# Decay sums of a gated-DeltaNet branch made once and laid out by DMA, with loads and block transfers issued by ScalarE

## What is computed

```python
gc = cumsum(g)                                     # inside the chunk
decay = exp(where(incl, gc[:, None] - gc[None, :], -inf))
kb = k * beta
lmat = where(strict, (kb @ k.T) * decay, 0)
sol = solve_unit_lower(lmat + I, concat([v * beta, kb * exp(gc)]))
u, w = sol[:, :dv], sol[:, dv:]
qk = where(incl, (q @ k.T) * decay, 0)
qg, kg = q * exp(gc), k * exp(gc[-1] - gc)
# per chunk, in order:
v_new = u - w @ s
o = qg @ s + qk @ v_new
s = s * exp(gc[-1]) + kg.T @ v_new
```

## Time and profile before

| | |
|---|---|
| median of 3 runs | 1328.33 us |
| lowest, highest | 1324.12, 1330.24 us |
| profiled execution | 1325.04 us, span 1322.7 us |
| PE busy | 1242.5 us (94% of the span) |
| DVE, ACT, POOL busy | 673.5, 294.7, 436.7 us |
| moved by DMA | 269.28 MB |

### The profile page before, as it was taken

The page is one execution under the profiler, slowest core; times in us unless marked ns, Lnnn a source line. Parts: engine busy times, 40 slices in busy tenths (PEclk is TensorE's granted clock), DMA queues, the critical chain, the costliest instruction groups (busy, mean ns, idle before and its releaser), DMA issues.

```text
span 1322.7 us, 20474 instructions
## 1 busy us (share of the span) xinstructions
PE 1242.5 (94%) x7131; PEld 635.1 (48%) x7131; DVE 673.5 (51%) x961; ACT 294.7 (22%) x650; POOL 436.7 (33%) x232
## 2 busy tenths in 40 slices
PE   6999999999989989999968887878999999999998
PEld 3444444455445444545535453334666644444443
DVE  3666305758878697684536653824442232543010
ACT  3111103333334433333312120001122221110000
POOL 1122203745444445444446654425441100000000
PEclk9999999999999999999989999998999999999999
DMA  7231508785875885877978998897778486242221
GB/s 232 93 109 38 165 0 276 232 257 171 274 259 171 263 277 176 268 244 229 312 217 279 288 309 304 288 264 239 232 241 265 146 271 234 82 150 69 91 64 64
DMA packets 171226, 269.28 MB, mean 204 GB/s; under 512 B 30010, under 2 KB 70849, under 8 KB 169964
## 3 DMA queue, kind: packets, MB, share of 16 engines
q1 hardware_dynamic: 148548, 216.83, 52.4%
q10 hardware_dynamic: 22576, 51.16, 10.8%
HBM read 221.66 MB, written 46.43 MB: 203 GB/s over the span
## 4 chain that ended last, share of the span: by engine, by line
PE 73%; SPq 10%; DVE 8%; issue 4%; DMA 3%; POOL 1%; ACT 1%; ACTq 0%; DVEq 0%; POOLq 0%
PE ps L1771 27%; PE ps L1686 9%; PE ps L2042 8%; PE ps L2067 8%; PE ps L1794 3%; PE ps L1821 3%; PE ps L1854 2%; SPq L496 2%; SPq L499 2%; PE ps L1883 2%; PE ps L1886 1%; SPq L437 1%; PE ps L1834 1%; DVE qkv L1357 1%; DMA work<-in_cache_v 1%
## 5 line engine op out<-in xcount | busy, mean ns | idle before, releaser
L1771 PE MATMUL ps<-hT,wbuf 128*128 128x512 f32 x1152 | 543.3, 607 | 0.0
L1771 PEld LDWEIGHTS ps<-hT,wbuf 128*128 128x128 f32 x1152 | 206.8, 193 | 202.3 <-issue 197.8
L767 POOL TENSOR_TENSOR prod<-work,qB 128x1024 f32<-128x1024 f32 x64 | 165.4, 2586 | 199.8 <-DMA work<-in_cache_k 119.1
L767 POOL TENSOR_TENSOR prod<-kbuf,qB 128x1024 f32<-128x1024 f32 x64 | 154.9, 2425 | 146.8 <-DVE sc L1311 70.5
L1311 DVE TENSOR_REDUCE sc<-prod 128x16 f32<-128x1024 f32 x128 | 154.2, 1211 | 46.6 <-POOL prod L767 45.9
L1686 PE MATMUL ps<-wbuf,hT 128*128 128x512 f32 x384 | 167.9, 595 | 0.3 <-ACT qkv L864 0.3
L1686 PEld LDWEIGHTS ps<-wbuf,hT 128*128 128x128 f32 x384 | 72.1, 190 | 87.7 <-issue 86.7
L2067 PE MATMUL ps<-hT,work 128*128 128x512 f32 x256 | 110.3, 592 | 0.0
L1794 PE MATMUL ps<-work,pr 128*2 128x128 f32 x2048 | 71.6, 274 | 16.3 <-DMA work<-in_cache_v 8.3
L2042 PE MATMUL ps<-qkv,wbuf 128*128 128x512 f32 x192 | 84.2, 593 | 0.0
L1794 PEld LDWEIGHTS ps<-work,pr 128*2 128x2 f32 x2048 | 45.3, 84 | 76.2 <-issue 55.8
(11 more groups left out here) (353 smaller groups left out, 1294.9 us busy)
## 6 DMA issues: line engine op xcount, KB each, us to landing
work<-in_cache_v SPq DMA_DIRECT2D x256, 256.0 KB, 3.5
kbuf<-in_cache_k SPq DMA_DIRECT2D x128, 256.0 KB, 3.3
work<-in_cache_k SPq DMA_DIRECT2D x128, 256.0 KB, 3.5
wbuf<-in_w_main ACTq DMA_DIRECT2D x10, 2048.0 KB, 12.2
feat_dram<-qkv ACTq DMA_DIRECT2D x20, 512.0 KB, 4.8
qkv<-in_x_prompt SPq DMA_DIRECT2D x16, 512.0 KB, 5.0
feat_dram<-fst ACTq DMA_DIRECT2D x32, 256.0 KB, 4.3
gsp<-work SPq DMA_DIRECT2D x12, 512.0 KB, 4.9
```

Source lines behind the costliest of these rows:

```text
L767: nc.gpsimd.tensor_tensor(prod[:, p % 4:p % 4 + 2, :], kpair[u], qB[:, j % 2:j % 2 + 1, :].to_broadcast([P, 2, W]), ALU.mult).then_inc(s[" ...
L1771: ins = nc.tensor.matmul(ps[:, 4 + n % 2, :], wbuf[:, wb, kk, f * P:(f + 1) * P], hT[:, kk, half_ * W:(half_ + 1) * W], start=(kk == 0), s ...
```

## The change

The sums of the decays are made once, ahead of the second attention head: PE makes suffix sums, totals, prefix sums by column (`gcol`, one value per partition) and prefix sums by row (`gcrow`) with four small matmuls; ACT evacuates them and stores the rows to `gc_dram`. For each chunk ACT loads the row of its four heads to all partitions (`gcB`, 128x512). ACT makes Dm = exp(-relu(gc_i - gc_j)) from `gcB` and `gcol`, four Relus and one exponential, and eG = exp(gcB). POOL's gU and PE's two decay matmuls go.

ACT issues the chunk loads (`gdn_load`), the load of the diagonal blocks, the store of the inverses and their four loads, which SP issued before. The plan's times change with it: 15 instead of 16 units per chunk, a larger share for the slots in that stage, and the inversion and solves follow.

```diff
     def keys_at(c, step=0):
 
-        return 465 + 16 * c + 1.4 * step
-
-    INVERT = keys_at(NT - 1, 19) + 5
+        return 465 + 15 * c + 1.4 * step
+
+    INVERT = keys_at(NT - 1, 16) + 5
 
     def solve_at(c):
-        return INVERT + 66 + 23.5 * c
+        return INVERT + 70 + 23 * c
 
     def scan_at(c):
         return solve_at(c) + 14
 
-    SHARE = ((440, 0.75), (keys_at(0), 0.95), (keys_at(NT - 1, 17), 0.34), (solve_at(0), 0.95), (solve_at(NT), 0.54), (2000, 0.95))
+    SHARE = ((440, 0.75), (keys_at(0), 0.95), (keys_at(NT - 1, 15), 0.45), (solve_at(0), 0.95), (solve_at(NT), 0.54), (2000, 0.95))
...
-        def gdn_load(c):
-            if c >= 3:
-                sp.wait_ge(s["kq_ready"], c - 2)
-                sp.wait_ge(s["qg_done"], c - 2)
-            for i in range(1, 4):
-                sp.dma_start(h3(Yt[c % 3][i]), feat_dram[i, :, :, PAD + c * P:PAD + (c + 1) * P].rearrange("g p n -> p g n")).then_inc(s[YIN[c % 3]], 16)
-
-            yield keys_at(c, -12)
-            if c == 0:
-                rows_stored(4 * AH)
-                sp.wait_ge(s["oaT_done"], AH)
-                for i in range(3):
-                    gdn_load(i)
-            yield keys_at(c, 5)
-            if 1 <= c and c + 2 < NT:
-                gdn_load(c + 2)
...
         def invert():
-            yield INVERT
+            yield INVERT + 2
             for u in range(2):
                 sp.wait_ge(s[f"g_st{u}"], STORED * NT // 2)
-            sp.dma_start(BN.rearrange("p j i -> p (j i)"), ld_dram.rearrange("c h b j i -> (c h b) (j i)")).then_inc(s["mask_in"], 16)
-            yield INVERT + 2
             for c in range(2):
                 scan_load(c)
-            yield INVERT + 55.6
-            sp.wait_ge(once("x_inv"), nth("x_inv"))
-            sp.dma_start(xd_dram.rearrange("e b i k -> (e b) (i k)"), XB.rearrange("p j i -> p (j i)")).then_inc(s["sp_st"], 16)
-            sp.wait_ge(s["sp_st"], 16 * 1)
-            rows_stored(ROWS)
-            for b in range(4):
-                sp.dma_start(Xc[32 * b:32 * b + 32], xd_dram[:, b].rearrange("e i k -> i e k")).then_inc(s["xc_in"], 16)
...
-            yield keys_at(c, -5)
-            if c == 0:
-                po.wait_ge(s["mask_in"], 32)
-                po.wait_ge(once("gb_done"), nth("gb_done"))
-                po.wait_ge(s["conv_done"], 3 * AH)
-            elif c >= 2:
-                po.wait_ge(s["gc_ready"], c - 1)
-            nc.gpsimd.tensor_tensor(h3(gU), bh4(upper), bc(gb[:, c, AH:8], P), ALU.mult).then_inc(s["gU_ready"], 1)
...
 
 
+        def decay_rows():
+
+            act.wait_ge(once("gcs_ready"), nth("gcs_ready"))
+            nc.scalar.activation(exal, ps[:, 3, 0:64], ACT.Exp)
+            nc.scalar.activation(gcol, ps[:, 3, 64:96], ACT.Copy).then_inc(once("exal"), 1)
+            nc.scalar.activation(gcrow, ps[0:64, 3, P:2 * P], ACT.Copy).then_inc(once("gcrow_evac"), 1)
+            act.wait_ge(once("gcrow_evac"), nth("gcrow_evac"))
+            act.dma_start(gc_dram, gcrow).then_inc(s["gcr_st"], 16)
+
         def attention(h):
 
...
+        def gdn_load(c):
+            if c >= 3:
+                act.wait_ge(s["kq_ready"], c - 2)
+                act.wait_ge(s["qg_done"], c - 2)
+            if c >= 2:
+                act.wait_ge(s["eG_ready"], c - 1)
+            elif c == 0:
+                act.wait_ge(s["conv_done"], 3 * AH)
+            act.dma_start(halves[c % 2][2], gc_dram[8 * c + AH:8 * c + 8].rearrange("(o h) n -> o (h n)", o=1).to_broadcast([P, W])).then_inc(s[f"gc_in{c % 2}"], 16)
+            for i in range(1, 4):
+                act.dma_start(h3(Yt[c % 3][i]), feat_dram[i, :, :, PAD + c * P:PAD + (c + 1) * P].rearrange("g p n -> p g n")).then_inc(s[YIN[c % 3]], 16)
+
+
...
+            ST, gsqr, (mS, eG), (kb, Dm, gcB) = STs[c % 2], gsqrs[c % 2], masks[c % 2], halves[c % 2]
+            yield keys_at(c, -1 if c == 0 else 0.5)
             if c == 0:
-                act.wait_ge(once("gcs_ready"), nth("gcs_ready"))
-                nc.scalar.activation(exal, ps[:, bank, 0:64], ACT.Exp).then_inc(once("exal"), 1)
+                for u in range(3):
+                    act.wait_ge(s[f"row_st{u}"], 16 * ((4 * AH - 1 - u) // 3 + 1))
+                act.wait_ge(s["oaT_done"], AH)
+                act.wait_ge(s["gcr_st"], 16)
+                for i in range(2):
+                    gdn_load(i)
             yield keys_at(c, 1.4)
             act.wait_ge(s["g1_tok"], c + 1)
             if c >= 2:
...
-            yield keys_at(c, 11.2)
-            act.wait_ge(s["E_ready"], c + 1)
+            yield keys_at(c, 4.6)
+            act.wait_ge(s[f"gc_in{c % 2}"], 16 * (c // 2 + 1))
             if c >= 2:
                 act.wait_ge(s["lq_done"], c - 1)
-            nc.scalar.activation(Dm, ps[:, bank, :], ACT.Exp).then_inc(s["Dm_ready"], 1)
+            for h in range(AH):
+                ins = nc.scalar.activation(Dm[:, h * P:(h + 1) * P], gcB[:, h * P:(h + 1) * P], ACT.Relu, bias=gcol[:, AH * c + h:AH * c + h + 1], scale=-1.0)
+            ins.then_inc(s["gap_ready"], 1)
+            act.wait_ge(s["g_mean"], c + 1)
+            nc.scalar.activation(eG, gcB, ACT.Exp).then_inc(s["eG_ready"], 1)
+            act.wait_ge(s["gap_ready"], c + 1)
+            nc.scalar.activation(Dm, Dm, ACT.Exp, scale=-1.0).then_inc(s["Dm_ready"], 1)
+            yield keys_at(c, 5.6)
+            if c == 0:
+                gdn_load(2)
+            if 1 <= c and c + 2 < NT:
+                gdn_load(c + 2)
+            yield keys_at(c, 11.2)
             act.wait_ge(s["kbt_ready"], c + 1)
             nc.scalar.activation(Yt[c % 3][0], ps[:, bank + 1, :], ACT.Copy).then_inc(s["kbT_ready"], 1)
-            yield keys_at(c, 13.2)
-            act.wait_ge(s["gc_ready"], c + 1)
-            nc.scalar.activation(eG, ps[:, bank, :], ACT.Exp).then_inc(s["eG_ready"], 1)
 
         def invert():
-            yield INVERT
+            yield INVERT + 5
+            for u in range(2):
+                act.wait_ge(s[f"g_st{u}"], STORED * NT // 2)
+            act.dma_start(BN.rearrange("p j i -> p (j i)"), ld_dram.rearrange("c h b j i -> (c h b) (j i)")).then_inc(s["mask_in"], 16)
+            yield INVERT + 59.1
+            act.wait_ge(once("x_inv"), nth("x_inv"))
+            act.dma_start(xd_dram.rearrange("e b i k -> (e b) (i k)"), XB.rearrange("p j i -> p (j i)")).then_inc(s["sp_st"], 16)
+            yield INVERT + 62.6
+            act.wait_ge(s["sp_st"], 16 * 1)
+            for u in range(3):
+                act.wait_ge(s[f"row_st{u}"], 16 * ((ROWS - 1 - u) // 3 + 1))
+            for b in range(4):
+                act.dma_start(Xc[32 * b:32 * b + 32], xd_dram[:, b].rearrange("e i k -> i e k")).then_inc(s["xc_in"], 16)
 
         def solve(c):
...
-            dve.wait_ge(s["kbt_ready"], c + 1)
+            dve.wait_ge(s["kbT_ready"], c + 1)
             nc.vector.tensor_tensor(ST[:, 0:512], tk, eG, ALU.mult).then_inc(s["kbg_done"], 1)
-            yield keys_at(c, 17.2)
+            yield keys_at(c, 14.6)
             dve.wait_ge(s["DmS_ready"], c + 1)
...
+                    if h == 1 and i == 0:
+                        pe.wait_ge(s["exp_done"], 16)
+                        pe.wait_ge(s["mask_in"], 32)
+                        pe.wait_ge(once("ring_free"), nth("ring_free"))
+                        gates = gb[:, 0:NT, AH:8]
+                        nc.tensor.matmul(ps[:, 3, 0:32], strict, gates, start=True, stop=True)
+                        nc.tensor.matmul(ps[:, 3, 32:64], ones[:], gates, start=True, stop=True)
+                        nc.tensor.matmul(ps[:, 3, 64:96], upper, gates, start=True, stop=True)
+                        nc.tensor.matmul(ps[0:64, 3, P:2 * P], gb[:, 0:NT, :].rearrange("p c n -> p (c n)"), upper, start=True, stop=True).then_inc(once("gcs_ready"), 1)
...
             yield keys_at(c, 11.2)
-            pe.wait_ge(s["gU_ready"], c + 1)
             pe.wait_ge(s["kg_done"], c + 1)
             tr_heads(kb, bank + 1).then_inc(s["kbt_ready"], 1)
+            yield keys_at(c, 13.2)
             pe.wait_ge(s["vB_done"], c + 1)
-            nc.tensor.matmul(ps[:, bank, :], strict, gU, start=True, stop=True).then_inc(s["E_ready"], 1)
-            yield keys_at(c, 12.4)
-            pe.wait_ge(s["Dm_ready"], c + 1)
-            nc.tensor.matmul(ps[:, bank, :], ones[:], gU, start=True, stop=True).then_inc(s["gc_ready"], 1)
-            yield keys_at(c, 16)
             pe.wait_ge(s["kbT_ready"], c + 1)
             pe.wait_ge(s["kbg_done"], c + 1)
```

40 lines of the change are left out of this document (20 added, 20 removed).

## The result

The changed kernel takes **1319.4 us** (median of 7 runs, 1310.2 to 1321.9) against 1329.3 for the kernel before: a ratio of **0.993**, with an interval of 0.991 to 0.995. It is faster by 10 us where 33 were forecast, and outside the range. A second set of runs of the same kernel, beside the last experiments (e14), gave 1319.9 us and again 0.993 (0.991 to 0.996). One execution of e7 ran at a granted clock of 0.655 and took 1813 us; ratios leave it out.

What follows compares the result with a forecast made beforehand. PE was taken as the bound from the first solve on, with SP's queue late before it. First solve -28 + 5, moved matmuls -10.5, attention +1 gave -32 from 1325.0, so 1293, plus 3.3 for the median: 1296 us, range 1280 to 1317.

Steps and rivals of the forecast that it cites:

- (a): PE loses two 512-column matmuls per chunk, worth 14 us; four small ones in the attention stage cost 1 us.
- (b): In each chunk, transpose of scaled keys to key product takes 3 us instead of 7.0, 4 less.
- (c): Start of the keys: SP no longer held, ACT issues the loads; first key product at 686 instead of 696.5.
- (d): Key chunks: SP stays the bound with 94 us over seven periods; last key product at 780 instead of 794.7.
- (e): From keys to inversion: DVE starts at 800 instead of 820.9; the 31 steps keep 46.1 us, ending at 846.
- (f): Inverse's store, loads and transpose with ACT issuing: 23.8 us, so first solve at 870 instead of 897.9.
- The warning of the step: In (f): weights ahead in ACT's ring may make the inverse's store take 11.3 us or more, not 9.8.
- (g): After the first solve 106 projection matmuls follow instead of 118, 10.5 us off where PE is the bound.
- (h): DMA engines from 660 to 890: 69.6 MB at 331 GB/s fits, with longer landings; charged 5 us, of 0 to 23.
- PE's idle stays: Rival: PE loses 50 us ahead of the first solve as before, solve at 894, total 1314; 0.22 shared with DMA-bound.
- DMA-bound: Rival: engines carry no more than 298 GB/s, first solve at 893, total 1314; 0.22 shared with PE's idle stays.
- ACT becomes the chain: Slower rival, in the chunks: ACT's issues and copies set the period; 1342 at 20 us a period; chance 0.05.

Runs made afterwards that it cites:

- e14: Second set of runs of the same changed kernel, nothing further changed, beside the last experiments: 1319.9 us, 0.993 against the kernel before.
- e7: Changed kernel, with SP holding its pages from 12 units ahead of the key chunks until chunk 0's three feature loads landed: 1319.5 us, 0.994.
- e3: Changed kernel with the plan's old numbers, 16 units per chunk and share 0.34: ratio 1.003 against the kernel before.
- e4: Changed kernel leaving work out: cache page loads within the key chunks bring 128 of 512 columns: 1316.4 us, 0.989 against the kernel before.
- e2: Changed kernel with the chunk loads (gate rows and features) given back to SP, new plan kept: ratio 1.003 against the kernel before.
- e13: Changed kernel with chunk loads and the inverse's trip back on SP and the plan's old numbers: ratio 1.006 against the kernel before.
- e1: Changed kernel with block load, inverse's store and its four loads back on SP, chunk loads staying on ACT: 1318.5 us, 0.992.
- e12: e6 leaving work out: cache pages issued between 42 and 76 units into the inversion bring 128 of 512 columns: 1314.6 us, 0.990.
- e5: Changed kernel with only the 2 MB weight load on ACT moved behind the inverse's four loads: 1315.7 us, 0.992 against the kernel before.
- e17: e3 with the inverse's store ahead of ACT's eviction and the 2 MB of weights at 75 units: 1319.0 us, 0.995 against the kernel before.
- e18: Kernel before, with ACT's 2 MB of weights moved from ahead of SP's inverse store to behind the four loads: 1320.1 us, 0.996.
- e15: e6 with the 2 MB of weights 75 units into the inversion, well behind the inverse's loads: 1312.6 us, 0.988 against the kernel before.
- e8: e6 with pages also held at the start: 1314.6 us, 0.992 against the kernel before.
- e6: e5 with the inverse's store also moved ahead of the feature eviction that waits for PE: 1312.5 us, 0.989 against the kernel before.

## Why the prediction was right and wrong

**(a) PE's work: right.** 13 us net were forecast, 11.8 measured. L1915 and L1918 are gone, and PE's busy time up to 668 us is 644.1 instead of 643.2.

**(b) The chunk's chain: right.** From the transpose of the scaled keys (696.0) to the key product (698.1) it takes 2.2 us, against 7.0 before and 3 forecast.

**(c) "The first key product starts at 686": wrong by 12.1 us.** In the kernel before SP issued the loads first and the pages after them; its standing still had kept the DMA engines free for them. Now SP issues fourteen pages from 658.8 to 677.6, and ACT the loads from 672.1 on. The first three landed in 7.3 us (median) instead of 4.1. The step had a price for the issue (up to 1.5 us) and none for the landing. Taken apart, the 12.1 us are: 2.4, by which DVE finished the last head later (670.5 and 668.1; 1.8 us of such a distance stand between the two executions at 77 us already); 1.9, in which ACT made and stored an eviction and loaded the decay row ahead of the first feature load; 4.9 more from that load to PE's transposes (11.1 and 6.2), of which e7 gives back 4.0 by holding the pages; and 2.9 more from there to the key product (14.6, and 11.6 in the forecast; 11.3 in e3, whose plan has two projection matmuls fewer there). Nor is SP free: it stands 15.5 us for the results of the first chunk, where before it stood 6.0 for the head and 2.8 for that chunk. The step was also worth little: the wait for the keys went (7.6), a wait for loads of 10.3 instead of 3.1 came, and e7 shows that shortening the latter does not reach the end.

**(d) The period: 14.2 us, forecast 13.4; wrong by 5.5 us over seven.** PE's work was right (82 forecast, 81.4 measured). The step took SP's 94 us as the bound, and the table under e4 bears that out: without its waits SP has 90.9 us there, and with 17 issues more (e2) the stage is 10.9 us longer. What the sum put at nothing are the 8.6 us in which SP stood for the chunks' results, 4.9 of them at once. PE's idle time is 18.2 us and not 12: 10.2 for the chunk's own chain (14.2 before), and 8.0 for value pages, for which it had not waited in that stretch before. That SP's issuing is what binds is read from these waits and from e2 and e13, which put the loads back; no run takes pages out of SP's order and leaves the rest.

**(e) "800 instead of 820.9": measured 822.0.** Of the 22, 17.7 come from (c) and (d), 4.3 are its own. The last block product ended at 800.9 and its store went out at 806.8, 5.9 us later, and not 1: SP's pages stand ahead of that store in its order, whoever issues the loads. The 31 steps took 49.4 us and not 46.1, since DVE stood 5.4 us in the middle of them for a page's product.

**(f) The trip, 23.8 us forecast, 34.6 measured.** Store 8.3 us behind the last step (4 forecast, 0 to 11.1), its landing 7.5 (9.8), the loads until the transpose 15.8 (7.0), and 3.0 as before. The term that failed is the loads. They were taken at their time on SP's queue, where SP issued nothing beside them because it waited; there e1 has them in 7.0 again, and with thin pages beside them e12 has them in 7.4 on ACT. The warning of the step, 2 MB ahead in ACT's ring, was true (e5), but the store came out shorter than in the kernel before, the loads twice as long. By the Trainium skill (DMA: Bandwidth & Descriptors, Queues, rings and completion order) one ring is consumed in order and an engine takes turns between the queues. The first agrees with the store's 14.0 us in e3 and 4.2 in e17. The prediction went on that on SP's ring the store did not wait for the weights, and there it was wrong: e18 shows that the 2 MB held up the store on the other queue too, 9.8 us instead of 4.4, so taking turns did not protect it.

**(g) Matmuls moved ahead: right.** 180.2 us from the first solve to the up-projection, 181 forecast, 191 before. The 35.9 us by which the first solve is late are (c) 12.1, (d) 5.5, (e) 7.5 with its steps, and (f) 10.8.

**(h) "It fits, with longer landings; I charge 5 us": this is the term that was mis-sized.** The bytes did fit, and e4 shows that fewer would have helped little. But the 5 us stood against everything that the fuller engines and the new order would cost ahead of the first solve, and that came to the 35.9 us of (g). The landings did grow. Over the keys' window, before and after: value pages 3.4 and 4.6 us, key pages in `work` 3.5 and 6.3, chunk loads (`ext`) 5.0 and 10.0, stores of scaled keys (`gsp<-work`) 5.2 and 6.5. They cost time where PE stood on one transfer: some 4 us at the first loads (e7) and 8.8 at the inverse's. In the keys' stage they did not set the time (e3, e2). The rest is order: SP's waits in (d), SP's pages ahead of a store in (e), ACT's evictions in (c) and (f).

How much of this reaches the end is open. No run brings back more than 7 of the 23 us between the forecast and the result (e15), and e8, with both the start and the trip changed, is no better than e6. The account by terms is of one execution each.

**The rivals.** Both middle ones gave 1314, 5 us from the result. "PE's idle stays" is the nearest to what happened: the chain's waits fell by 9 us, and more of others came (of the waits listed above, 48.5 us before and 58.7 after). "DMA-bound" had the right symptom (0.99) and the wrong mechanism, since the rate was no ceiling (361 GB/s in e3, 0.989 in e4). The Trainium skill's sentence on issuing from several engines (DMA: Bandwidth & Descriptors, Issuing engines are not separate DMA queues), which the prediction set aside because SP's issue time was full, is half borne out: for the inverse's trip it was worth nothing (e1), for the chunk loads, where SP's issuing was full, about 13 us (e2). "ACT becomes the chain" did not happen in the chunks, though three loads took up to 4.3 us to issue there; at the trip its order cost about as much as SP's had.

## What to carry to other kernels

While SP stood still on a wait here, the DMA engines were free for what it waited for. Before such a wait is taken away, ask what its queue will then put beside the transfers of the critical path, and price their landing by rows in which the queues are full, not by those of the idle queue. A longer landing costs only where the bound engine stands on it, though: in the keys' stage landings grew, some to the double, and the time still followed what SP had to issue. So count the issues of the busiest queue, and add the waits in which it stands between them. Balance the bound engine's work against its idle time, and forecast the two apart: here its work was right to 1 us, and the idle time was off by 28 in the profiled executions. A small transfer that everything waits for should have no large one in flight ahead of it, be it on another queue; moving 2 MB out of its way was worth 5 us in the kernel before. In the changed one it was 2 (e5, within the intervals), and 5 to 7 together with an earlier place for the store (e6, e15).

## What the runs showed that was not expected

- The time of the issue itself is not constant, and it was longest with much in flight: four loads of 128 KB took 2.7 us on SP in the kernel before, 6.4 on ACT in the changed one, 9.2 in e3 right behind 2 MB, and 2.9 in e12. One feature store's issue, 0.33 us otherwise, took 4.65 right behind the loads:

```profile
894.27 4.65 ACTq L958 DMA_DIRECT2D feat_dram<-fst  x1
```

- 2 MB on one queue more than doubled the landing of a 512 KB store on another (9.8 and 4.4 us, e18).
- 3.5 MB of loads on SP's queue kept its pages from PE for about 11 us, in two places 34 us apart.
- Waits for pages did not follow the bytes: with three tenths less in the stage they went from 8.0 to 7.2 us.
